# Two reorderings of VectorE's queue in a hybrid encoder kernel: mLSTM weights ahead of the attention's squares and sums, and one chunk's denominators ahead of two additions

## The reference

```
h = rmsnorm(x); [aq ak av | sz sxbc sdt | mq mk mv mo mi mf] = h @ W_in
x = x + concat(window_gqa_attention, bidirectional_ssd, bidirectional_mlstm) @ W_out
x = x + expert_choice_swiglu_moe(rmsnorm(x))
```

```
wq  = exp(dmat - m_l) * (q k^T)                 # "weights", per head and direction
num = wq @ v + (q @ c_prev) * sc
den = max(|sum(wq) + (q @ n_prev) * sc|, exp(-m_l))
h_f or h_b = num / den
h = rmsnorm(h_f + h_b);  out = sigmoid(o) * h
```

## Time and profile before

| | us |
|---|---|
| median of 3 runs (lowest, highest) | 2426.39 (2426.32, 2428.22) |
| the profiled execution | 2424.09 |
| its span, first to last instruction | 2422.6 |
| TensorE matmul busy | 2337.5 (96%) |
| VectorE busy | 1049.0 (43%) |
| ScalarE busy | 584.8 (24%) |
| GpSimd busy | 530.0 (22%) |

### The profile page before, as it was taken

One profiled execution on the slowest core, in us unless ns is written; L12 is line 12 of the kernel. 1 busy time (PEld: TensorE's weight loads), 2 busy tenths in 40 slices (PEclk: granted clock), 3 DMA queues, 4 the chain that ended last, 5 costly groups with the idle time before them and its releaser, 6 DMA issues.

```text
span 2422.6 us, 34266 instructions
## 1 busy us (share of the span) xinstructions
PE 2337.5 (96%) x13634; PEld 1683.0 (69%) x13634; DVE 1049.0 (43%) x1965; ACT 584.8 (24%) x1267; POOL 530.0 (22%) x544
## 2 busy tenths in 40 slices
PE   7999999999998999999889999999999999999997
PEld 4577578874545788877645775888745468887885
DVE  4851565596545111111148515655965541111111
ACT  3220232344332111111132212323433421111110
POOL 1011453143201111111110214531432011111111
PEclk9999999999999999999999999999999999999998
DMA  3102222121227888778331022312212288878882
GB/s 130 38 18 68 82 90 71 62 96 53 79 79 278 305 289 281 266 262 289 93 115 38 18 70 70 105 53 70 88 56 76 79 318 305 285 253 280 282 282 44
DMA packets 149344, 352.24 MB, mean 145 GB/s; under 512 B 9885, under 2 KB 38049, under 8 KB 149186
## 3 DMA queue, kind: packets, MB, share of 16 engines
q1 hardware_dynamic: 134210, 308.11, 35.4%
q0 software_dynamic: 14976, 41.95, 7.0%
HBM read 307.75 MB, written 42.28 MB: 144 GB/s over the span
## 4 chain that ended last, share of the span: by engine, by line
PE 85%; DVE 7%; ACT 2%; DMA 2%; POOL 1%; issue 1%; SPq 1%; DVEq 0%; POOLq 0%; ACTq 0%; PEldq 0%
PE ps L1682 80%; DVE SCR L1121 1%; PE ps L2220 1%; ACT SCR L967 1%; PE ps L1973 1%; DVE MID L1247 1%; PE ps L2035 1%; DMA SCR<-cs_rows 1%; DVE TMP L1121 1%; PE ps L1698 1%; DMA SCR<-m_rows 1%; DVE SCR L1130 1%; DVE TMP L1511 0%; DVE HT L1121 0%; PE ps L1891 0%
## 5 line engine op out<-in xcount | busy, mean ns | idle before, releaser
L1682 PE MATMUL ps<-MID,HT 128*128 128x512 f32 (+2 forms) x2240 | 605.7, 497 | 2.9 <-PE ps L1682 2.9
L1682 PE MATMUL ps<-HT,MID 128*128 128x160 f32 (+2 forms) x4192 | 575.3, 304 | 6.5 <-DVE HT L1121 3.7
L1682 PEld LDWEIGHTS ps<-HT,MID 128*128 128x128 f32 (+1 forms) x4192 | 560.4, 189 | 27.5 <-issue 27.0
L1682 PE MATMUL ps<-RING,HT 128*128 128x256 f32 (+2 forms) x2080 | 466.7, 391 | 2.5 <-DVE RING L1125 1.3
L1682 PEld LDWEIGHTS ps<-RING,HT 128*128 128x128 f32 (+1 forms) x2080 | 371.8, 190 | 86.8 <-issue 37.1
L1682 PEld LDWEIGHTS ps<-MID,HT 128*128 128x128 f32 (+1 forms) x2240 | 231.2, 151 | 228.0 <-issue 208.2
L1682 PE MATMUL ps<-HT,RING 128*128 128x512 f32 (+1 forms) x960 | 351.9, 524 | 0.0
L1130 DVE SCALAR_TENSOR_TENSOR HT<-HT,ps 128x160 f32<-128x160 f32 (+1 forms) x128 | 40.9, 319 | 704.9 <-ACT HT L1090 677.5
L1682 PEld LDWEIGHTS ps<-HT,RING 128*128 128x128 f32 x960 | 180.2, 190 | 159.7 <-issue 152.0
L795 POOL DMA_INDIRECT y_prompt<-SCR,idxp x32 | 50.6, 1581 | 664.7 <-ACT SCR L1108 645.1
L1090 ACT ACTIVATE HT<-ps 128x160 f32<-128x160 f32 (+1 forms) x128 | 38.7, 302 | 520.7 <-PE ps L1682 509.8
(11 more groups left out here) (236 smaller groups left out, 2175.6 us busy)
## 6 DMA issues: line engine op xcount, KB each, us to landing
MID<-w_gate SPq DMA_DIRECT2D x32, 2048.0 KB
MID<-w_up SPq DMA_DIRECT2D x32, 2048.0 KB
MID<-w_down SPq DMA_DIRECT2D x32, 2048.0 KB, 15.2
RING<-w_in SPq DMA_DIRECT2D x22, 1024.0 KB, 5.4
SCR<-cs_rows SPq DMA_DIRECT2D x20, 1024.0 KB, 5.3
SCR<-m_rows SPq DMA_DIRECT2D x20, 512.0 KB, 3.9
MID<-w_out SPq DMA_DIRECT2D x8, 1024.0 KB, 6.8
y_sample<-RING SPq DMA_DIRECT2D x16, 512.0 KB, 2.6
```

The lines of the kernel that those rows point to most:

```text
L1682: return pe.matmul(out, a, b, start=start, stop=stop)
```

## The change

Only VectorE's queue changes, in both layers. In the mLSTM loop `ml_weights(c + 1)` now stands ahead of `attn_product` or `attn_sum`. Later, `attn_den(2)` stands ahead of `keep_y(1, 2)` and `add_x(0, 1)` instead of behind them.

```diff
@@ -1448,13 +1448,13 @@
                             keep_y(0, 0)
                         if c >= 1:
                             ml_output(c - 1)
+                        if c + 1 < NC:
+                            ml_weights(c + 1)
                         if 1 <= c <= 8:
                             if c % 2:
                                 attn_product(c // 2)
                             else:
                                 attn_sum(c // 2 - 1)
-                        if c + 1 < NC:
-                            ml_weights(c + 1)
 
                     ml_read(NC - 1)
                     keep_turned(1)
@@ -1547,9 +1547,9 @@
                     keep_turned(4)
                     attn_square(5)
                     keep_y(1, 1)
+                    attn_den(2)
                     keep_y(1, 2)
                     add_x(0, 1)
-                    attn_den(2)
                     attn_square(6)
                     for n in range(1, NC - 2):
                         if n > 1:
```

## The result

The prediction was wrong. The median of 16 runs is **2436.26 us** (2430.76 to 2440.45), beside 2428.04 us (2426.32 to 2431.78) for 16 runs of the kernel before: a ratio of 1.003, 95% interval 1.0023 to 1.0038. That is 8.2 us slower, where 1.6 were forecast, and it lies above the range. The profiled execution took 2434.29 us around a span of 2432.8.

What follows compares the result with a forecast made beforehand. VectorE was taken to bound the mLSTM loop, at 7.7 us a chunk, with TensorE leading the chain overall. The terms +3.8 and -2.2 gave +1.6 us, so 2428.0 us; range 2424.0 to 2431.8.

Steps and rivals of the forecast that it cites:

- Step (a): mLSTM loop, iteration 1: VectorE's square, free before its wait for ScalarE, now comes after it; +0.6 us per layer.
- Step (b): mLSTM loop, iterations 2, 4, 6: later sum delays GpSimd's root and mask 0.62 us; VectorE waits 0.45 us, three times, +1.35.
- Part 2: Output projection start: denominators ahead of two additions let GpSimd's third scale start earlier; gain 1.1 us per layer, 2.2 in all.
- h: Time point in the mLSTM loop, the end of the mLSTM reduction, from which root, mask and exponentials were timed.
- Rival 3: Output projection: the denominators' move gains nothing, as VectorE's square delays scores and residual work; +3.8 us, 2430.2; 12%.
- rival 2: mLSTM loop: GpSimd's lateness is absorbed by slack in ScalarE or the loads; -1.0 us, 2425.4; 18%.
- rival 4: Loops: TensorE's 4.7 us of waits on VectorE go, since weights come 0.6 us earlier; -6.9 us, 2419.5; 3%.
- the interlock: mLSTM loop: VectorE's gate instructions slowed beside GpSimd's mask pair, 0.25 + 0.31 = 0.56 us, taken as unchanged.
- Part 1: mLSTM loop: weights ahead of squares and sums on VectorE; no gain, cost +3.8 us over both layers.
- Rival 1: mLSTM loop: each moved mask holds VectorE for its whole 0.70 us, 1.41 per even iteration; +6.7 us, 2433.1; 12%.

Runs made afterwards that it cites:

- p2_den_first: Kernel before with only the denominators (`attn_den(2)`) moved ahead of the two additions: 2422.87 us, ratio 0.999; the same kernel repeated: 2424.65 us, ratio 0.9992.
- after_filled_two: Changed kernel plus two idle TensorE matmuls of 256 columns in iterations 2, 4, 6 and 8 of the mLSTM loop: 2426.39 us, ratio 1.0003.
- p1_weights_first: Changed kernel with the denominators' move undone, so only weights ahead of squares and sums: 2435.84 us, ratio 1.0033.
- before_long_waits: Kernel before with VectorE's 128x384 square made twice in iterations 3, 5 and 7: 2431.04 us, ratio 1.0022.
- after_again: The changed kernel itself, unaltered, run again beside the filled kernel: 2436.18 us, ratio 1.004.

## Why the prediction was wrong

**Right.** Step (a): the square stands behind the wait, +0.6 us. Step (b): GpSimd 0.66 us late (0.62 forecast), three waits of 0.43 (0.45). Part 2: the 1.54 us gone, 0.40 left for the scores. Counted from h, root and mask landed within 0.05 us of where they were put. Rival 3 (part 2 gives nothing) falls by p2_den_first, and so does rival 2, by the 0.43 us waits; rival 4 falls by TensorE's waits on VectorE, which grew to 7.4 us.

**A little off.** "Taken as unchanged" was the interlock, at 0.56 us a mask pair. It moved, in both directions. In the kernel before the gate and the 128x8 instruction behind it take 0.68 + 0.74 + 0.17 = 1.59 us in even iterations (481.18) and 1.33 in odd ones (488.91). Now it is 0.42 + 0.87 + 0.49 = 1.78 in even ones (482.78) and 1.18 in odd ones (491.22). The square, too, takes 0.68 us behind the weights instead of 0.56. A pair of iterations so became 15.75 us instead of 15.20, 0.55 longer rather than 0.45. And part 2 gained 0.75 us a layer, not 1.1. With these sizes, and with both layers like layer 0, the sum would have been 2 x (0.6 + 3 x 0.55 - 0.75) = +3.0 us instead of +1.6, still within 0.2%. Part 1 is 4.5 us of it, where the drop-free loops show 5.2 and 3.8 were forecast. after_filled_two, which has all of this and no drop, measured +0.7, -2.2 to +3.6. Rival 1, the whole GpSimd instruction blocking VectorE (the Trainium skill, "SBUF — State Buffer", Who interferes with whom), would be 1.41 us; the rows don't bear it out for the masks. That its 2433.1 us lies nearer to the measured time than the forecast is chance. The square of chunk 7, though, started 1.07 us into the scale and ended 0.41 us behind its end (570.91 and 570.50), so for that long instruction the trace agrees with the rule.

**The step that failed** is one that the sum left out: where the prediction says that in this loop "VectorE is the bound" and that "TensorE waits for it, 0.4 us at a time", TensorE's idle time was costed at what it is, and its length at nothing. Both numbers were also averages over two kinds of iteration: 7.7 us is the longer of two distances (493.47 to 501.20; the one before it, 486.00 to 493.47, is 7.47), and 4.7 by 11 hides a 0.17 beside a 0.42. VectorE's reads (`ml_read`, the 128x520 instructions on PSUM) show it, in the kernel before and then in the changed one:

```profile
479.71 0.70 DVE L1121 TENSOR_TENSOR TMP<-ps,small 128x520 f32<-128x520 f32 x1
...
487.44 0.70 DVE L1121 TENSOR_TENSOR TMP<-ps,small 128x520 f32<-128x520 f32 x1
```

```profile
481.32 0.70 DVE L1121 TENSOR_TENSOR TMP<-ps,small 128x520 f32<-128x520 f32 x1
...
489.76 0.70 DVE L1121 TENSOR_TENSOR TMP<-ps,small 128x520 f32<-128x520 f32 x1
```

In the kernel before they start 7.73 us apart over an even iteration's gate (479.71 to 487.44) and 7.47 over an odd one's (487.44 to 494.91); TensorE waits 0.42 after the one and 0.17 after the other. Now it is 8.44 us (481.32 to 489.76) and 7.31 (to 497.07). From iteration 2 on, everything that the change adds falls in the interval that was the longer one: 0.43 of waiting, 0.19 of interlock, 0.12 of the square, 0.71 in sum with the gaps. TensorE's wait behind it goes from 0.42 to 1.14; its wait behind the other, from 0.17 to nothing. The mean has grown by little, the single wait almost threefold. The granted clock falls after about half of such waits, and a drop costs more than its wait: TensorE's work takes 3.3 us longer at 510 (a unit 2.52 and small matmuls 0.77), 3.3 at 497 in p1_weights_first (2.63 and 0.67), 1.6 at 492 in before_long_waits (1.41 and 0.22). With the same waits of VectorE and TensorE's gap filled, 9.8 us of the loss were gone (after_filled_two against after_again): that is what the step left out. A drop was in the prediction only as 1.1 us, once in the upper bound of the range and once inside a rival of 12%, where interlock came on top. Even the drop before, from which the 1.1 comes, cost TensorE 1.6 us (a unit of 5.07 instead of 3.72 at 1683.47, small matmuls of 1.39 instead of 1.11). A drop should have been a rival of its own, and the rows for it were there: a drop in layer 1 before follows a wait of 0.65 us, and from step (b) it could be worked out that the 0.45 us come on top of the longer of TensorE's two waits, 0.42 + 0.45 = 0.87, and not evenly.

The size fits roughly. If the mean clock is made of its two levels (an estimate), 2427 us at 0.9888 hold 2 x 0.0112 x 2427 = 54 us at the lower one, and 2436 at 0.9858 hold 69. These 15 us more at half speed cost TensorE 7 to 8 us, where it is the one who leads; with +0.7 to +3.0 for the order that gives 8 to 11 us, and 8.2 were measured. after_filled_two has 51 us by the same working, against 72 of the changed kernel beside it: 10 us, and 9.8 were measured. It is an upper estimate, as TensorE doesn't lead everywhere: p1_weights_first would come to 8.1 + 4.5 = 12.6 us and measured 8.5, before_long_waits to 6.4 + 3.5 = 10 and measured 4.0 to 5.3.

**Open.** Which of the waits is followed by a drop: that of 1.14 us at 491.34 was not and the equal one at 507.09 was. In the fourteen profiles (both kernels and the twelve runs) each wait of TensorE before a chunk's sum in the two loops (none, where filling matmuls stand right ahead of it) can be set beside the unit that follows:

| wait before the sum, us | sums | with a slowed unit behind them (4.8 us or more instead of 3.72) |
|---|---|---|
| under 0.47 | 179 | 0 |
| 0.47 to 0.79 | 27 | 5 |
| 0.80 to 0.95 | 12 | 5 |
| 0.96 and over | 18 | 9 |

So a longer wait is more often followed by a drop, but its length alone doesn't decide, and no run here shows what else does.

How much of the difference lies outside the loops is partly answered by the same profiles. The two loops together take 167.9, 173.1 and 174.6 us in the three profiles with all of part 1's order and nothing filled or moved (the changed kernel, after_again, p1_weights_first), and 160.6 and 160.7 in the two with part 2 alone. That is 11 us on average, and the medians of the changed kernel and of part 2 alone lie 11.5 to 13.4 us apart; so most of part 1's loss is in the loops, as far as three profiles that scatter by 7 us can tell. The stretch between the two loops takes 1123 to 1131 us, whichever the kernel, and the one ahead of the first 453 to 459.

No version beats the kernel before by much. Part 2 alone is the best, at 0.999 and 0.9992.

## What to carry to other kernels

Where TensorE is busy 95% of the time, its idle time has a length as well as a sum. An edit on another engine that turns two waits of 0.2 and 0.4 us into one of 1.1 can cost three times the wait (3.3 us), so count what a reordering adds to each interval between two of the reads that TensorE waits for, and not only their sum, and spread it. If an order is wanted anyway, two idle matmuls in the gap are a cheap test of whether the clock is the cause (here 10 us). And a loss found this way shows in the mean granted clock over many runs before it shows in a profile's chain, which here read 84% TensorE instead of 85%.

## What the runs showed that was not expected

- A drop of TensorE's granted clock follows some of the single waits of 0.48 to 1.15 us in stretches where it is otherwise busy nearly all of the time, 9 of 18 at 0.96 us and over and none of 179 under 0.47. In all 19 drops read in these loops the slowed unit is the one right behind a sum that had waited so long (1680.25, then 1683.47, in the kernel before; 507.09, then 510.81, in the changed one). A unit of 3.72 us then takes 4.8 to 6.4.
- Two matmuls of 128x256 on constants, in a group of 1.13 us, keep the clock at 1.00 over both loops in the profile, with one wait of 0.89 us left unfilled (1693.23), and the time falls by 9.8 us though nothing is computed with them. The kernel before already has such matmuls in the choice of tokens (`keep_clock`).
- Four of them (rows of 1.99 us) are more than the gap holds: with the clock at 1.00 all the same, the ratio is 1.0022 instead of 1.0003.
